# Forgetting attention's rows and keys in one order, beside three tiles of its key projection; state space's input weights split by halves

## The reference, cut to what matters

```python
for l in range(DEPTH_2):                       # 2 layers
    x = post_add(x, swiglu(pre(x, 0), ...), 0, 0.5)
    y = token_mixer(pre(x, 1), ...)
    x = post_add(x, y, 1, 1.0)
    x = post_add(x, swiglu(pre(x, 2), ...), 2, 0.5)

def token_mixer(h, w_in, ...):
    u, q, k, v, f, g_a, g_b = split(h @ w_in)  # u, q, k, v 512 wide, f 8
    y_a = glu(gelu(s5_ssm(u, ...)))
    y_b = forgetting_attention(q, k, v, f + forget_b) @ attn_w_out
    return (sigmoid(g_a) * y_a + sigmoid(g_b) * y_b) @ w_out
```

## Time and profile before

| | us |
|---|---|
| median of 3 runs (3500.5 to 3505.64) | 3502.28 |
| the profiled execution | 3502.85 |
| its span, first to last instruction | 3501.0 |
| TensorE busy | 3400.4 |
| VectorE busy | 1624.9 |
| ScalarE busy | 1232.8 |
| GpSimd busy | 432.5 |
| mean granted clock of TensorE | 0.988 |

### The profile page before, as it was taken

How to read it: one execution, slowest core, us unless ns; L and a number is a source line. 1 busy time by engine, 2 the same in 40 slices (tenths; PEclk the granted TensorE clock), 3 DMA queues, 4 the chain that set the end, 5 groups by cost and what they waited for, 6 DMA issues and landing times.

```text
span 3501.0 us, 38941 instructions
## 1 busy us (share of the span) xinstructions
PE 3400.4 (97%) x16278; PEld 2655.7 (76%) x16278; DVE 1624.9 (46%) x2118; ACT 1232.8 (35%) x1772; POOL 432.5 (12%) x338
## 2 busy tenths in 40 slices
PE   7998999999999999999999999999999999999998
PEld 6754477688888888887578788878888775878886
DVE  5555566443335635464234534475455533352233
ACT  3365465432223332224533322233323246332222
POOL 0100012112220100112011100110101210210001
PEclk9999999999999999999999999999999999999999
DMA  5411653233332333223032344433432321222221
GB/s 188 138 49 43 183 185 145 91 141 140 141 140 106 119 135 134 85 105 118 19 108 102 124 142 145 138 119 108 149 102 67 127 91 51 94 75 99 93 95 60
DMA packets 78352, 393.41 MB, mean 112 GB/s; under 512 B 8417, under 2 KB 17121, under 8 KB 45025
## 3 DMA queue, kind: packets, MB, share of 16 engines
q1 hardware_dynamic: 66048, 370.41, 30.8%
q10 hardware_dynamic: 12128, 20.52, 1.6%
HBM read 372.02 MB, written 18.87 MB: 112 GB/s over the span
## 4 chain that ended last, share of the span: by engine, by line
PE 91%; DVE 4%; ACT 3%; issue 1%; DMA 0%; POOL 0%; SPq 0%; DVEq 0%; ACTq 0%; POOLq 0%
PE pb L678 22%; PE pb L680 22%; PE pb L679 22%; PE pb L585 3%; PE pb L646 2%; PE pb L647 2%; PE pb L654 2%; PE pb L583 2%; PE pb L840 1%; PE pb L858 1%; PE pb L710 1%; PE pb L821 1%; DVE wl L1946 1%; PE pb L1188 1%; ACT wh L1281 1%
## 5 line engine op out<-in xcount | busy, mean ns | idle before, releaser
L1946 DVE TENSOR_TENSOR wl<-w,wh 128x2048 fp32r<-128x2048 f32 (+2 forms) x266 | 586.8, 2206 | 923.1 <-ACT wh L1281 920.8
L678 PE MATMUL pb<-XH,wh 128*128 128x512 f32 (+1 forms) x2488 | 984.0, 396 | 3.5 <-DVE wl L1946 2.8
L680 PE MATMUL pb<-XH,wl 128*128 128x512 f32 (+1 forms) x2488 | 970.2, 390 | 0.0
L679 PE MATMUL pb<-XL,wh 128*128 128x512 f32 (+1 forms) x2488 | 970.0, 390 | 0.0
L1281 ACT ACTIVATE wh<-w 128x2048 fp32r<-128x2048 f32 (+2 forms) x266 | 475.4, 1787 | 278.7 <-PE pb L680 195.0
L678 PEld LDWEIGHTS pb<-XH,wh 128*128 128x128 f32 (+1 forms) x2488 | 465.9, 187 | 110.4 <-issue 8.2
L679 PEld LDWEIGHTS pb<-XL,wh 128*128 128x128 f32 (+1 forms) x2488 | 466.0, 187 | 101.1 <-issue 4.5
L680 PEld LDWEIGHTS pb<-XH,wl 128*128 128x128 f32 (+1 forms) x2488 | 465.7, 187 | 100.7
L2860 POOL TENSOR_TENSOR HL<-tmps,HH 128x512 fp32r<-128x512 f32 x120 | 165.8, 1384 | 1318.8 <-ACT HH L1590 1318.8
L678 PE MATMUL pb<-HH,wh 128*128 128x512 f32 x768 | 306.6, 399 | 0.0
L680 PE MATMUL pb<-HH,wl 128*128 128x512 f32 x768 | 303.7, 395 | 0.0
(11 more groups left out here) (468 smaller groups left out, 4061.4 us busy)
## 6 DMA issues: line engine op xcount, KB each, us to landing
w<-in_f_in SPq DMA_DIRECT2D x88, 1024.0 KB, 5.0
mreg<-in_mod_w SPq DMA_DIRECT2D x144, 512.0 KB, 3.6
w<-in_f_out SPq DMA_DIRECT2D x32, 1024.0 KB, 5.0
w<-in_w_up SPq DMA_DIRECT2D x16, 1024.0 KB, 5.7
w<-in_w_dn SPq DMA_DIRECT2D x16, 1024.0 KB, 5.7
w<-in_m_g SPq DMA_DIRECT2D x16, 1024.0 KB, 5.0
w<-in_f_out SPq DMA_DIRECT2D x16, 768.0 KB, 4.2
w<-in_w_rm SPq DMA_DIRECT2D x8, 1024.0 KB, 5.7
```

The costliest lines, as they stand in the source:

```text
L678: mm(dst, hi[:, cs], xh[:, k, :], start=k == 0, stop=False)
L679: mm(dst, hi[:, cs], xl[:, k, :], start=False, stop=False)
L680: x = mm(dst, lo[:, cs], xh[:, k, :], start=False, stop=fin)
L1946: tt(low[:, 0:s.cols], wslots[b % 3][:, 0:s.cols], h[:, 0:s.cols].bitcast(F32), ALU.subtract).then_inc(*DV.up(("lo", b), ("w_free", b)))
```

## The change

FOX_STEPS gets an entry ("j", 0), one third of a tile of the key projection, and is put together anew: tile 0, then row steps 0 to 9 with nine such parts between them, the first turn, row steps 10 and 11, key steps 0 to 3 alternating with row steps 12 to 15, the second logarithm, key steps 4 to 6, the second turn, key steps 7 to 17. The first logarithm stands before row step 8. All steps with a pair of banks share one ring of three in the order of the list (`FOX_RING`, `fox_pair`, `fox_free`), and the second turn takes a place in it. The first block of `("ao", l)` is split at ("h", 0), behind key step 9.

In `plan`, the first block of the stage that follows a wide stage computed as four tiles at once (`v`, `("u", l)`) is split ahead of that stage's first eviction, not of its third.

State space's second input block is split by halves of 1024 columns. ScalarE takes one before the last square of the feed-forward before it, one before the link's first root; VectorE one before it waits for that root, one before the first scaling.

```diff
+FOX_STEPS = [("j", 0)] * 3
+for _n in range(10):
+    FOX_STEPS += [("f", 0)] * (_n == 8) + [("s", _n)] + [("j", 0)] * (_n != 6)
+FOX_STEPS += [("r", 0), ("s", 10), ("s", 11)]
+for _n in range(4):
+    FOX_STEPS += [("t", _n), ("s", 12 + _n)]
+FOX_STEPS += [("f", 1), ("t", 4), ("t", 5), ("t", 6), ("r", 1)]
+for _n in range(7, 18):
+    FOX_STEPS += [("t", _n)] + [("h", 0)] * (_n == 9)
+
+FOX_RING = [_x for _x in FOX_STEPS if _x[0] == "s" or _x == ("r", 1) or _x[0] == "t" and _x[1] < 16]
...
-            elif nx is not None and not nx.raw:
-                st.ahead[g, 0].append((nx, 1 if nx.extra else 0))
+            elif nx is not None and not nx.raw and st.name[0] != "mk":
+                st.ahead[0 if st.four and st.wide else g, 0].append((nx, 1 if nx.extra else 0))
...
+        def fox_pair(*step):
+
+            b = 2 + 2 * (FOX_RING.index(step) % 3)
+            return [banks[b], banks[b + 1]]
...
+            def fox_free(l, *step):
+
+                i = FOX_RING.index(step)
+                if i >= 3:
+                    what, n = FOX_RING[i - 3]
+                    pe.wait_ge(*(at("rows_low", l, n) if what == "r" else at("row_sum" if what == "s" else "weights", l, n, 1)))
...
             def key_scores(l, n):
...
-                pe.wait_ge(*(at("weights", l, n - 3, 1) if n >= 3 else at("row_sum", l, (15, 13, 14)[n], 1)))
+                fox_free(l, "t", n)
...
             def key_values(l, n):
                 pr, kb = n // 4, n % 4
-                if n == 4:
-                    pe.wait_ge(*at("rows_low", l, 1))
...
-                run(st_of[("mk", l)], XH, XL)
+                job = gemm(st_of[("mk", l)], XH, XL)
                 for what, n in FOX_STEPS:
-                    if what == "s":
+                    if what == "j":
+                        next(job)
+                    elif what == "s":
...
+            def hi_half(s, g, half):
+
+                b, i, cs = s.b[g], s.split[g], slice(1024 * half, 1024 * half + 1024)
+                begun.add(b)
+                if half == 0:
+                    act.wait_ge(w_landed[b % 3], 16 * (b // 3 + 1))
+                    act.wait_ge(*at("split_free", i - 2))
+                actf(whl[i % 2][0][:, cs], wslots[b % 3][:, cs], ACT.Copy).then_inc(*AC.up(("hi_half", b, half), ("hi", b)))
...
             def link(r, nxt):
 
                 mc = modc[3 * nxt[0] + nxt[1]]
+                if nxt[1] == 1:
+                    hi_half(st_of[("u", nxt[0])], 1, 1)
                 root(r if r == "final" else ("y", r), 512, 3, 2)
                 act.wait_ge(*at("ms", nxt))
                 actf(rnext, ms, ACT.Sqrt, bias=c("eps")).then_inc(*AC.up(("root", ("pre", nxt))))
-                if nxt[1] == 1:
-                    hi(st_of[("u", nxt[0])], 1)
...
                         if q == 2:
+                            if j == 7 and f == 0:
+                                hi_half(st_of[("u", l)], 1, 0)
                             (last_square if r == (1, 2) else y_square)(r, j, at("y_new", i, j))
...
                 name = r if final else ("y", r)
+                if nxt[1] == 1:
+                    lo_half(st_of[("u", nxt[0])], 1, 0)
                 dve.wait_ge(*at("root", name))
...
                 v.reciprocal(rnext, rnext).then_inc(*DV.up(("inverse", ("pre", nxt))))
+                if nxt[1] == 1:
+                    lo_half(st_of[("u", nxt[0])], 1, 1)
                 dve.wait_ge(*at("spread", name))
...
-                    if k == 2 and nxt[1] == 1:
-                        lo(st_of[("u", nxt[0])], 1)
```

More of the change, by code:

```diff
@@ L430, in fox_bank, with turn_bank @@
             return banks[(st_of[("ao", l)].o[0][0] + pr) % 2]
+        def fox_pair(*step):
+            b = 2 + 2 * (FOX_RING.index(step) % 3)
+            return [banks[b], banks[b + 1]]
+        def turn_bank(l, half):
+            return fox_pair("r", 1)[0] if half else fox_bank(l, 0)
         def stat(pr, i, par):
@@ L1159, in row_scores @@
                     pe.wait_ge(*at("ncol", l))
-                pair = [banks[2 + 2 * (m % 3) + par] for par in range(2)]
-                if m >= 3:
-                    pe.wait_ge(*at("row_sum", l, m - 3, 1))
+                fox_free(l, "s", m)
+                pair = fox_pair("s", m)
                 for par in range(2):
@@ L1174, in turn_rows @@
                 pe.wait_ge(*at("shift", l, half))
+                if half:
+                    fox_free(l, "r", half)
                 for i in range(4):
-                    x = nc.tensor.transpose(fox_bank(l, half)[0:4, i * 128:(i + 1) * 128],
+                    x = nc.tensor.transpose(turn_bank(l, half)[0:4, i * 128:(i + 1) * 128],
                                             sh[:, 16 * half + 4 * i:16 * half + 4 * i + 4], c("ident"))
@@ L1182, in key_scores @@
                 q0 = 128 * kb
-                pair = [banks[2 + 2 * (n % 3) + par] for par in range(2)]
+                pair = fox_pair("t", n)
                 if kb == 0 and pr % 2 == 0:
                     pe.wait_ge(*at("rows_low", l, pr // 2))
-                pe.wait_ge(*(at("weights", l, n - 3, 1) if n >= 3 else at("row_sum", l, (15, 13, 14)[n], 1)))
+                fox_free(l, "t", n)
                 for par in range(2):
@@ L1822, in _ @@
                 actf(ncol, banks[4][:, 0:32], ACT.Copy).then_inc(*AC.up(("ncol", l)))
-                run(st_of[("mk", l)], copy_scaled(k2, 1.0))
+                job = evict(st_of[("mk", l)], copy_scaled(k2, 1.0))
                 for what, n in FOX_STEPS:
-                    if what == "s":
+                    if what == "j":
+                        next(job)
+                    elif what == "h":
+                        hi(st_of[("ao", l)], 0)
+                    elif what == "s":
                         pr, i = n // 4, n % 4
@@ L1947, in lo, with lo_half @@
                     *DV.up(("lo", b), ("w_free", b)))
+            def lo_half(s, g, half):
+                b, cs = s.b[g], slice(1024 * half, 1024 * half + 1024)
+                begun.add(b)
+                dve.wait_ge(*at("hi_half", b, half))
+                h, low = slot(s, g)
+                tt(low[:, cs], wslots[b % 3][:, cs], h[:, cs].bitcast(F32), ALU.subtract).then_inc(
+                    *DV.up(*([("lo", b), ("w_free", b)] if half else [])))
             def evict(s, fn, ahead=True):
@@ L2750, in _ @@
                        ALU.subtract).then_inc(*DV.up(("crow", l)))
-                run(st_of[("mk", l)])
+                job = evict(st_of[("mk", l)], None)
                 for what, n in FOX_STEPS:
-                    if what == "s":
+                    if what == "j":
+                        next(job)
+                    elif what == "h":
+                        lo(st_of[("ao", l)], 0)
+                    elif what == "s":
                         pr, i = n // 4, n % 4
```

12 lines of the change are left out of this document (5 added, 7 removed).

## The result

The changed kernel takes **3490.69 us** (median of 7 runs, 3487.33 to 3493.92) against 3502.3 (7 runs, 3496.91 to 3505.64): the ratio is 0.9967, with a 95% interval of 0.9956 to 0.9979. It was run once more on another chip as an experiment, 3489.9 against 3502.31, 0.9964 [0.9952, 0.9977]. The profiled execution took 3492.85, 10.0 less than the profiled one of before, and its span is 3490.9.

A forecast was written before the change was run, and what follows sets the result against it. TensorE, busy 97% of the span, bounds the kernel, so gains come from idle or low-clock time. Attention 5.6, halves 3.1 and narrow splits 2.1 sum to 10.8 us off 3502.85; forecast 3492.0, range 3486.5 to 3499.5.

The forecast's parts named there:

- The stage as a whole: Forgetting attention, key tile 0's end to output projection: gains 2.0 us in layer 0, 3.6 in layer 1, together 5.6.
- The waits, one by one: Forgetting attention: TensorE would wait for evictions, turned rows and exponentials, from 0.3 us (key step 0) to 3.25 (value product 4).
- The first logarithm: Between row steps 7 and 10: 2.9 us of table loads and logarithm hidden by some 6 us of TensorE work.
- Insertions: Nine key projection parts among row steps: 0.1 us each for changing shape, 0.7 a layer after overlap, bounds 0 and 1.5.
- The clock: Forgetting attention, behind value product 4's wait: clock falls to the lower level, costing 2.3 us a layer, bounds 0 and 4.
- The link: State space weights split by halves: gain 1.06 us in layer 0, nearly 2.27 in layer 1; a clock fall loses layer 0 0.3.
- Narrow splits: Gates' wait 0.82 us and forget column's two 0.17 gone, turn's wait 0.25 and 0.65 shorter: sum 2.1.
- The output projection's split: Its first weights' split, moved behind key step 9, would cost 0, at most 0.2 us.
- A: Rival: clock stays up behind the second logarithm, 2.3 us less in each layer; 3488 us, chance 0.13.
- D: Rival: clock, once fallen at value product 4, stays low through the remaining key steps; 3520 us, chance 0.05.
- C: Rival: ScalarE can't switch tables with work in flight, 1.28 us more per uncovered load; 3497 us, chance 0.05.
- B: Rival: the wait only moves, with longer and further clock falls; gain 4 to 5 us, 3498 us, chance 0.20.

The follow-up runs named there:

- experiment 2: Changed kernel with all four key projection tiles ahead of row step 0, none of their parts among the row steps: 3501.86 us, ratio to before 0.9996.
- all three edits: Changed kernel with a third of key tile 1 before row step 0, second turn behind key step 4, VectorE's second half behind normed tile 0: 3488.99 and 3487.52 us.
- Experiment 1: Changed kernel with only the new order of forgetting attention; state space halves and earlier narrow splits undone: 3497.79 us, ratio to before 0.9989.
- experiment 6: Changed kernel with a copy in place of each layer's second logarithm, so no table switch there: 3482.12 us, a single execution.
- experiment 3: Changed kernel with the halves undone, so the link's state space weights are split whole as before: 3500.39 us, a single execution.

## Why the prediction was right, and which of its steps were not

The forecast of 3492.0 is 1.3 us above the 3490.7, which lies in the range; the working holds in part. The total is closer than its parts: by the medians the order gave 4.4 us for a forecast 5.6, the halves and the narrow splits 7.1 for 5.2, and that the two errors cancel is luck.

- **The stage as a whole.** From key tile 0's end I forecast 73.8 us in both layers; without that tile's 5.4 it is 73.0 and 75.7, in the second profile 74.2 and 74.2. The gain of 5.6 came as 4.7 and 5.0.
- **The waits, one by one** (forecast, measured): row step 0 0.85, 0.73; key step 0 0.3, none; row step 12 and key step 1 0.9, 0.84; value product 4 3.25, 3.19; key step 8 1.5, 1.43. But for key step 0, chains of durations off the old timeline gave the waits to 0.12.
- **The first logarithm** is covered, and experiment 2 shows by what: the parts of the projection.
- **Insertions** were the term that was mis-sized. The changed kernel's timeline (1678.47 to 1680.70 and the next parts) gives 0.31 in place of 0.23 from a part's first matmul to its second, and 0.32 in place of 0.23 from its last to the row step: 0.17 each, some 1.5 us a layer where I had 0.7. It lies at my upper bound and about cancels what the waits were less than forecast.
- **The clock** I priced at 2.3 us a layer. The windows hold 3.4 and 10.2 us of low time, and 6.8 and 6.8 in the second profile: 1.5, 4.5, 3.0 and 3.0. The average is 3.0, above what I took, and one of the four is outside my bound of 4; no row could have said which. My own sum already had that nearly all of layer 0's gain is clock (54.6 us for the old stage at full clock, 55.0 for the new), and I did not draw the conclusion: that this gain lasts only if the falls do not come somewhere else. For the order they did not (81 us of low time in the mean against 95); for all three edits some of them did.
- **The link**: forecast 1.06 and 2.27. The two halves stand where they were put (1498.68 and 1501.99 on VectorE, 1.22 and 1.20 us), and TensorE's wait grew to 2.01, as forecast (2.1). Link lengths against before: 0.8 and 2.0 us less, 1.6 and 2.3 in the second profile. "If it falls, layer 0 loses 0.3": it fell in one profile and not in the other, and even then 0.8 was won, since a fall costs 1.5 and I had taken nearly the whole gain and 0.3 more.
- **Does it arrive?** Against the one profile of before it seems not to: from the link to the next key tile the stretches of layers 0 and 1 together are only 1.7 and 1.0 us shorter, where 4.3 was forecast for link, forget column and turn, and their low time is 20.5 us against 10.2. But that profile was lucky just there. Experiment 1 runs the same instructions in these stretches as the kernel before, and takes 350.6 us for the two (27.3 of low time) where the profile of before has 345.1 and the changed kernel 343.4 and 344.1. Against experiment 1 the gain is 7.2 and 6.5. So the 5.2 us forecast for halves and narrow splits arrived, 7.1 by the medians, 5.0 of the mean at full clock. What this sum lacked is any price for falls outside of attention and layer 0's link: some 2 us of the gain are such falls.
- **Narrow splits**: the waits of the turn of u fell by 0.20 and 0.61 (forecast 0.25 and 0.65), and the wait of the gates is gone. The first block shows 1.0 to 2.0 rather than 0.82, of which I can't explain the excess. Low-clock luck in the stretches without an edit is a further 0.7 in the first profile (4.3 in the second). The output projection's split, priced at 0, cost nothing in layer 0: TensorE waits for none of its weights.
- **Rivals.** A (clock stays up) falls: 0.53 behind the wait. D (clock stays low) falls: the window that starts at 1730.70 is back at 1.00. C falls: in this timeline nothing drains around a table load, 0.01 to 0.02 us between the loads and their neighbours, while the Trainium skill ("ScalarE: Activation LUTs", What ACT_TABLE_LOAD costs) adds some 1380 ns; the measurement decides, as it did in the rows before. B (the wait only moves) did not give its time, but its mechanism is there: layer 1 has a second fall behind the wait of 1.43, and the link of layer 0 had one.

## What to carry to other kernels

Waits of one or two microseconds between matmuls are worth removing for their own length; what the falls of the clock add on top is not a property of the place. Price a stage at full clock and its low time apart, and check the gain on stretches that were not edited: with all three edits 10 us of a stage came back in stretches that compute the same thing. Then take the mean clock of many executions: in layer 1's link and state space the one profile of before had 6.8 us of low time where experiment 1 had 17.1 with the same instructions, and by that profile alone most of the gain there would have been missed, while over all executions the low time fell by 19 us and was most of what the change is worth. A short job of steady matmuls cut into parts covers a chain on ScalarE (table load, logarithm, table load) at 0.17 us a part.

## What was not expected of the hardware

- A fall of the granted clock isn't tied to a wait of a given length. A wait of 2.01 us was followed by a fall in one profile of the changed kernel and by none in the other; a wait of 1.43 left the clock alone in layer 0, and was followed by a fall in layer 1 (2921.16, a first group of 1.54 instead of 1.13) and in experiment 6. With all three edits the wait of 2.06 us at layer 0's second turn had one behind it in the first profile and none in the second. And the link behind layer 1's attention ran at 1.00 or at 0.64 with the same instructions.
- The low time of the whole kernel hardly follows its waits: 75.1 us before, 71.7 and 64.9 in the changed kernel, 78.5 and 75.1 with all three edits, although TensorE's waits in the two attentions went from 14.9 to 12.4 and 6.2 us. The means over all executions (95, 76 and 84 us) follow the waits for the change and not for the three edits. The spread of one and the same kernel goes with the clock: of the ten runs of experiment 1, 3493.37 to 3503.53, the fastest has a mean clock of 0.990 and the slowest 0.987. Why it moves with the edits stays open; no run here separates it.
- Two profiles with all three edits, on two chips, show the same falls at the same places behind layer 1's attention (3054.6, 3095.6 and 3471.1; 3053.2, 3094.2 and 3469.6), and experiment 3 has them too (3066.1, 3107.0, 3482.5), where the changed kernel has none or one. So it isn't noise of a single execution either.
